# The inverse steps of a recurrent layer as 64x64 tiles on two diagonal quadrants of TensorE

## The reference, cut to what matters

```python
def step(s, inp):                       # one token, all heads, s is 64x64 per head
    r_t, w_t, k_t, v_t, kk_t, a_t = inp
    sa = jnp.einsum('bhij,bhj->bhi', s, -kk_t)
    s = (s * w_t[:, :, None, :]
         + sa[..., None] * (kk_t * a_t)[:, :, None, :]
         + v_t[..., None] * k_t[:, :, None, :])
    return s, jnp.einsum('bhij,bhj->bhi', s, r_t)
```

## Time and profile before

| | |
|---|---|
| median of 3 runs | 5675.57 us |
| the profiled execution | 5675.5 us |
| its span, first to last instruction | 5673.7 us |
| granted TensorE clock, mean | 0.89 |
| first product, all six turns (line 1301) | x1200 matmuls, 168.3 us busy |
| second product (line 1309) | x1200 matmuls, 160.3 us busy |
| transposes (line 1317) | x480, 72.0 us busy |
| subtraction on VectorE (line 1486) | x150, 688 ns each |

### The profile page before, as it was taken

How to read it: one execution, slowest core, us unless ns; L and a number is a source line. 1 busy time by engine, 2 the same in 40 slices (tenths; PEclk the granted TensorE clock), 3 DMA queues, 4 the chain that set the end, 5 groups by cost and what they waited for, 6 DMA issues and landing times. The chain is left out here.

```text
span 5673.7 us, 72170 instructions
## 1 busy us (share of the span) xinstructions
PE 4543.2 (80%) x24898; PEld 3776.1 (67%) x24898; DVE 3798.9 (67%) x6648; ACT 1526.8 (27%) x2454; POOL 2309.9 (41%) x1748
## 2 busy tenths in 40 slices
PE   3677869779678754999999948787884499999995
PEld 0356758658556744999999944433574499999994
DVE  1144453443524986999999972341498699999997
ACT  0122213212211133333333321110113333333332
POOL 0022312412301486566666640000148656666664
PEclk8779879789789877999999979878997799999997
DMA  9110000000011025999999951101102499999996
GB/s 389 47 50 14 1 14 1 14 14 1 2 64 67 1 59 171 388 398 406 404 397 406 405 183 58 54 19 64 67 1 59 143 394 393 406 406 398 407 403 225
DMA packets 382991, 1049.09 MB, mean 185 GB/s; under 512 B 36647, under 2 KB 168999, under 8 KB 376616
## 3 DMA queue, kind: packets, MB, share of 16 engines
q0 software_dynamic: 147456, 536.94, 24.1%
q1 hardware_dynamic: 235368, 509.88, 24.0%
HBM read 990.62 MB, written 56.07 MB: 184 GB/s over the span
## 5 line engine op out<-in xcount | busy, mean ns | idle before, releaser
L733 PE MATMUL bank<-h_parts,u_parts 128*128 128x384 f32 x6144 | 1116.8, 336 | 97.1 <-DVE u_parts L808 97.1
L733 PEld LDWEIGHTS bank<-h_parts,u_parts 128*128 128x128 f32 x6144 | 1083.0, 188 | 116.9 <-issue 97.5
L743 PE MATMUL bank<-v_parts,gg_parts 128*128 128x512 f32 x4608 | 1095.7, 391 | 0.0
L705 POOL DMA_INDIRECT u_rows<-in_u_rows,rows_idx x512 | 696.3, 1360 | 767.1 <-DVE dots L812 680.2
L743 PEld LDWEIGHTS bank<-v_parts,gg_parts 128*128 128x128 f32 x4608 | 861.2, 188 | 170.5
L818 DVE SCALAR_TENSOR_TENSOR rows_y<-v_rows,row_scale,rows_y 128x1024 f32<-128x1024 f32 x512 | 660.5, 1291 | 29.9 <-DMA v_rows<-in_peer_v,rows_idx 15.6
L711 POOL DMA_INDIRECT v_rows<-in_peer_v,rows_idx x512 | 609.3, 1190 | 168.7 <-issue 150.6
L812 DVE CUSTOM_DVE_ANT_0 u_rows<-u_rows,rows_h 128x1024 f32<-128x1024 f32 x512 | 622.0, 1215 | 0.0
L604 DVE TENSOR_TENSOR hot<-selT,iota 128x1024 f32<-128x1024 f32 x192 | 376.8, 2038 | 34.2 <-PEq L618 34.2
L302 POOL TENSOR_TENSOR x<-x,gb 128x1024 f32<-128x1024 f32 x20 | 46.9, 2346 | 831.7 <-ACT x L295 831.7
L613 POOL TENSOR_TENSOR hot<-hot,selT 128x512 f32<-128x512 f32 x192 | 377.7, 2004 | 10.9 <-DVE hot L604 10.9
(11 more groups left out here) (302 smaller groups left out, 6497.1 us busy)
## 6 DMA issues: line engine op xcount, KB each, us to landing
hT<-in_peer_u SPq DMA_DIRECT2D x260, 512.0 KB, 8.3
v_in<-in_peer_v SPq DMA_DIRECT2D x256, 512.0 KB, 6.5
w_modt<-in_w_mod SPq DMA_DIRECT2D x24, 2048.0 KB, 23.0
gates<-gates_sb SPq DMA_DIRECT2D x6, 8192.0 KB, 30.4
g_in<-gates SPq DMA_DIRECT2D x256, 192.0 KB, 7.9
wq<-in_peer_wq SPq DMA_DIRECT2D x32, 512.0 KB, 11.4
w_hy<-in_hy_w_in SPq DMA_DIRECT2D x9, 1536.0 KB, 6.6
w_rkv<-in_w_rkv SPq DMA_DIRECT2D x6, 1536.0 KB, 6.6
```

The source lines that it names most:

```text
L705: pool.indirect_dma_start(ug[n % GR][:, :], None, m.i["u_rows"], bass.IndirectOffsetOnAxis(ap=R.idx[:, n % 2, n // 2:n // 2 + 1], axis=0)) ...
L733: mm = pe.matmul(m.bank[j % 2][:, 0:TD], us[:, j % 2, a, k, :], hs[:, b, k, :], start=(k == 0 and i == 0), stop=(k == KD - 1 and i == 2))
L743: mm = pe.matmul(yb[t][c][:, :], gs[:, j, a, t * P:(t + 1) * P], vs[:, j % 2, b, c * BANK:(c + 1) * BANK], start=(first and i == 0), stop= ...
```

## The change

Each of a unit's 128x128 matmuls becomes two 64x64 matmuls, one for each diagonal block, b = 0 on rows and columns 0 to 63 of TensorE and b = 1 on rows and columns 64 to 127. Each quadrant has its own bank: the first product writes banks 3 and 4 for even units and 5 and 6 for odd ones, the second product banks 7 and 0. The second product's banks are so the same for every unit, and TensorE now waits for the subtraction of the unit just before (`rk_xt` at TT + u), not of the one before that. The copy to `T1` and the subtraction from `XT` become two instructions of 64 partitions x 256 elements each, in place of one of 128 x 512. The blocks off the diagonal are no longer multiplied, copied or subtracted. The transposes stay 128x128.

```diff
                             for dh in range(4):
-                                mm = pe.matmul(m.bank[5 + n % 2][:, dh * P:(dh + 1) * P], LM[:, n % LM_RING, dh], X[:, t, dh], start=True, stop=True)
+                                for b in range(2):
+                                    r = slice(CH * b, CH * b + CH)
+                                    mm = pe.matmul(m.bank[3 + 2 * (n % 2) + b][r, dh * CH:(dh + 1) * CH], LM[r, n % LM_RING, dh, r], X[r, t, dh, r],
+                                                   start=True, stop=True, tile_position=(CH * b, CH * b))
                             mm.then_inc(s["rk_t1"], 1)
                         if 1 <= n <= UNITS:
                             u = n - 1
                             pe.wait_ge(s["rk_t1sb"], u + 1)
-                            if u >= 2:
-                                pe.wait_ge(s["rk_xt"], TT + u - 1)
+                            if u >= 1:
+                                pe.wait_ge(s["rk_xt"], TT + u)
                             for dh in range(4):
-                                mm = pe.matmul(m.bank[(7, 0)[u % 2]][:, dh * P:(dh + 1) * P], T1[:, u % 3, dh], XT[:, u % TT, dh], start=True, stop=True)
+                                for b in range(2):
+                                    r = slice(CH * b, CH * b + CH)
+                                    mm = pe.matmul(m.bank[(7, 0)[b]][r, dh * CH:(dh + 1) * CH], T1[r, u % 3, dh, r], XT[r, u % TT, dh, r],
+                                                   start=True, stop=True, tile_position=(CH * b, CH * b))
                             mm.then_inc(s["rk_t2t"], 1)
...
-                            act.activation(T1[:, n % 3].rearrange("p a b -> p (a b)"), m.bank[5 + n % 2][:, :], ACT.Copy).then_inc(s["rk_t1sb"], 1)
+                            for b in range(2):
+                                r = slice(CH * b, CH * b + CH)
+                                ins = act.activation(T1[r, n % 3, :, r], m.bank[3 + 2 * (n % 2) + b][r, 0:4 * CH].rearrange("p (a b) -> p a b", a=4), ACT.Copy)
+                            ins.then_inc(s["rk_t1sb"], 1)
...
-                        dve.tensor_tensor(XT[:, n % TT], XT[:, n % TT], m.bank[(7, 0)[n % 2]][:, :].rearrange("p (a b) -> p a b", a=4), ALU.subtract).then_inc(s["rk_xt"], 1)
+                        for b in range(2):
+                            r = slice(CH * b, CH * b + CH)
+                            ins = dve.tensor_tensor(XT[r, n % TT, :, r], XT[r, n % TT, :, r], m.bank[(7, 0)[b]][r, 0:4 * CH].rearrange("p (a b) -> p a b", a=4), ALU.subtract)
+                        ins.then_inc(s["rk_xt"], 1)
```

## The result

The changed kernel takes 5726.72 us (median of 4 runs, 5718.58 to 5728.08) against 5676.59 us before: ratio 1.0086, interval 1.0069 to 1.0104. It is slower by about 50 us. I had forecast 5603, so the change went the other way.

The account below looks back on a forecast made before the run. The prediction took TensorE to bound the inverse stage; passes, tail and start would save 9.7 + 0.6 + 1.7 = 12.0 us a turn, 72 us in six, from 5675.5 to 5603 us. Range 5578 to 5655 us, chance 0.83.

Parts of the forecast that it names:

- What bounds the stage: Inverse stage: TensorE feeds the rest, its pass of 2.23 us full, while ScalarE, GpSimd and VectorE wait on it.
- two tiles side by side: Both products: the two quadrants run in parallel, 0.058 us an entry, so a product takes 0.46 us instead of 0.89.
- Rival A: Products: the quadrants take turns, a product takes 0.93 us and a pass 2.65; 5734 us, slower; chance 0.07.
- B: Products: a quadrant's weights load only after its own matmul, 0.107 us an entry, pass 2.51; 5715 us; chance 0.04.
- Changing the shape: Each pass: TensorE going from 128x128 transposes to 64x64 tiles and back costs 0.35 us, bounds 0 to 0.8.
- The full pass: Inverse stage: a pass takes 1.71 us against 2.224, saving 9.7 us a turn over 19 passes.
- The start: Start of the inverse stage, at 1.2 GHz: gain of 1.7 us a turn, between 0 and 2.5.
- VectorE: Subtraction in two halves: 0.33 us start to start plus 0.42, 0.75 in place of 0.69, hidden behind TensorE.
- The tail: Last units, no transposes hiding the new wait: second products step by 1.51 us three times; still 0.6 us gained.
- what the stage saves should shorten the turn: End of the inverse stage: the scan starts 0.05 us after the last subtraction, so stage savings, 12.0 us, shorten each turn.
- Rival C: Inverse stage: the clock falls to 1.2 GHz throughout, a pass takes 3.2 us; 5790 us; chance 0.02.
- Rival D: VectorE's way 0.3 us longer: passes lose 1 us a turn, the tail 0.9; 5614 us, inside the forecast's 0.83.

Follow-up runs that it names:

- e10: e9 plus idle 128x128 identity matmuls in TensorE's waits ahead of the inverse stage; 5555.52 us, ratio 0.9788.
- e8: Changed kernel with both quadrants of a second product in one bank, units alternating between banks 7 and 0; 5586.89 us, ratio 0.9844.
- e2: Changed kernel with idle quadrant identity matmuls in TensorE's waits of passes 23 to 25 and before the scan; 5608.85 us, ratio 0.9883.
- e5: Changed kernel with idle quadrant matmuls only in the last wait before the scan; 5609.21 us, ratio 0.9881.
- e6: Changed kernel with idle quadrant matmuls only in the waits of passes 23, 24 and 25; 5606.56 us, ratio 0.9877.
- e4: Changed kernel with second products of units 22 and 24 in banks 1 and 2, which the transposes leave free; 5600.21 us, ratio 0.9868.
- e1: Kernel before the change, with three more VectorE copies ahead of each turn's last subtraction; 5793.7 us, ratio 1.0209.
- e9: e8 with each transpose as two 64x64 matmuls against the identity; 5583.41 us, spread 5563.64 to 5634.32, ratio 0.9851.

## Why the prediction was wrong

- *What bounds the stage, and two tiles side by side:* right. A quadrant's entry is 0.52 / 8 = 0.065 us with its share of a change of shape, 0.058 without (e10), where 0.111 was the step of the whole array. Rival A is refuted. So is B, since load and stream in a row would make 0.107; the rule that I weighed for it, of the Trainium skill's page "TensorE: Matmul & The Clock Gate", section "Part 3: Packing small matmuls — row/col tiling", that weight loads overlap running matmuls only when the row group differs, is not borne out here: within a quadrant the row group is the same, and an entry takes 0.058. That the measured 5727 us lies near the prices of A (5734) and B (5715) is chance.
- *Changing the shape:* close. 0.35 us forecast; e8 and e10 put it at about 0.31, and the rest of the changed kernel's excess went with the banks.
- *The full pass:* 1.71 forecast, 1.72 measured, (426.13 - 393.44) / 19, between the last two of these rows of the changed kernel's timeline, the transposes of units 0 and 19; the first row is the stage's start:

```profile
388.18 1.97 PE L1303 MATMUL bank<-early 64*64 64x64 f32 x32 [3.01 <-DVE early L1491]
393.44 0.77 PE L1323 MATMUL bank<-ident,XT 128*128 128x128 f32 x4
426.13 0.66 PE L1323 MATMUL bank<-ident,XT 128*128 128x128 f32 x4
```

  9.7 us a turn forecast, 42.25 - 32.69 = 9.6 measured. The start, 388.18 to 393.44, is 5.26 in place of 7.12: 1.9 gained, 1.7 forecast.
- *VectorE:* mis-sized. The two halves took 0.85 us, not 0.75: the second starts only when the first has ended, unlike the 0.33 step of the earlier trace rows. In the passes it stayed hidden.
- *The tail:* the steps were 1.72, not 1.51. Of the 0.21 more, 0.10 is VectorE's and the rest the way to it and back. From unit 19's transposes to the scan is 434.01 - 426.13 = 7.88, where it was 7.69: in place of a gain of 0.6, a loss of 0.2. In sum 11.2 us a turn, where I had 12.0; the six stages of the two traces say 65.8 / 6 = 11.0.
- **The step that failed** is the sentence "what the stage saves should shorten the turn". I worked out the tail's waits, priced them at their own length, and never asked what they do to the clock of the stage behind them. They cost 14.5 to 15.6 us in each of five turns and 41.7 in the last, 115 us against the 66 that the stage gained. e2, e5 and e6 give them back by filling the waits, e4 and e8 by removing them, and e1 takes them from the old kernel by a wait alone.
- *Rival C* had the mechanism at the wrong place: I tested it where the new work runs (there the clock stayed at 1.00) and gave it 0.02. *Rival D* had the wait at the right place and priced only its length. Neither asked what the two make together.
- *The rows that should have warned me* are the kernel's own. TensorE waits 1.00 us at 362.76 and then once more:

```profile
366.28 0.48 PE L1287 MATMUL bank<-ident,region 128*128 128x128 f32 x1 [1.39 <-DVE region L1472]
```

  In the trace before, the granted clock is 1.00 from 360.0 to 365.2 and 0.50 from there to the start of the inverse stage, where the earlier trace rows shows it. So two waits hardly longer than the tail's had come before a fall already. A bound for its price stood there too, an estimate from the stretch of the last turn's scan: TensorE is busy 57.53 us in it, and twice as long at half the clock would be 57.5 more (41.7 measured).

## What to carry over

When a change makes TensorE faster in one stage, look at the waits that it opens at the end of it, and price the *next* stage at the lower clock level; here a chain of dependent matmuls lost more than the stage before it had gained. Where a wait can't be removed (another bank, another order), matmuls that nobody reads can stand in it; in e2, e5 and e6 they cost nothing. 64x64 tiles on the diagonal paid for block-diagonal 32-bit products, most with everything around them in the same shape.

## What was not expected of the hardware

- Four waits of 0.57 to 1.03 us within six, or one of 2.16 after dense work (e1), came before a fall to 1.2 GHz. It lasted about 31 us in the first turn (27 in e1's), and in the last turn, which has no pieces of a next turn between its steps, the 110 us to the end of the scan; what brings the clock back wasn't tried. Waits of 0.40 and 0.95 in e8 did not lose it in six turns; 0.25 and 0.95 in e9's first turn did, and in its second didn't.
- Two diagonal 64x64 tiles write the two partition halves of one PSUM bank side by side (e8: 0.56 us a product).
- Going from 128x128 to 64x64 tiles and back costs about 0.31 us a pair of changes here (e8 against e10), two thirds of a 64x64 product's 0.46.
- Neither engine overlapped the two halves of its split operation: ScalarE's two 64x256 copies from PSUM take 0.77 us (0.38 each), where one of 128x512 took 0.60, and VectorE's two subtractions 0.85 (0.42 each), where one took 0.69.
